# Weaving the FFN's activations and residual in 16-byte chunks

## The reference

```python
x = x + merged @ w_o                                   # D_MODEL = 2048
h = rmsnorm(x, norm_ffn_g)
z = h @ w_up                                           # D_FF = 5632, two halves
a, v = z[..., :D_FF], z[..., D_FF:]
ext = jnp.concatenate([buf, a], axis=1)                # buf: the last 2 rows
conv = conv_b + sum(conv_w[k] * ext[:, k:k + T] for k in range(3))
x = x + (jax.nn.silu(conv) * v) @ w_down
y = rmsnorm(x, norm_final_g)
```

## Time and profile before

| | us |
|---|---|
| median of 3 runs | 1944.33 (1944.02 to 1944.99) |
| the profiled execution | 1944.88 |
| its span, first to last instruction | 1943.1 |
| PE busy | 1927.0 (99%) |
| DVE busy | 1091.2 (56%) |
| ACT busy | 760.4 (39%) |
| POOL busy | 96.4 (5%) |

### The profile page before, as it was taken

The page is one execution under the profiler, slowest core; times in us unless marked ns, Lnnn a source line. Parts: engine busy times, 40 slices in busy tenths (PEclk is TensorE's granted clock), DMA queues, the critical chain, the costliest instruction groups (busy, mean ns, idle before and its releaser), DMA issues.

```text
span 1943.1 us, 34161 instructions
## 1 busy us (share of the span) xinstructions
PE 1927.0 (99%) x13412; PEld 1909.0 (98%) x13412; DVE 1091.2 (56%) x1506; ACT 760.4 (39%) x846; POOL 96.4 (5%) x252
## 2 busy tenths in 40 slices
PE   9999999999999999999999999999999999999997
PEld 8999999999999999999999999999999999999997
DVE  6865344434345774455556565656656556565656
ACT  5456542332257653333343333332323333333334
POOL 0002000000000350000000000000000000000000
PEclk9999999999999999999999999999999999999999
DMA  7444444444443697454444444434344444443443
GB/s 254 152 152 178 151 151 151 151 151 151 151 173 136 214 312 257 166 205 151 151 159 152 141 163 141 162 140 162 139 163 151 151 151 151 139 163 138 165 145 112
DMA packets 60042, 318.18 MB, mean 164 GB/s; under 512 B 6674, under 2 KB 6994, under 8 KB 27346
## 3 DMA queue, kind: packets, MB, share of 16 engines
q1 hardware_dynamic: 59330, 313.15, 45.0%
q10 hardware_dynamic: 656, 4.27, 0.5%
HBM read 313.08 MB, written 4.32 MB: 163 GB/s over the span
## 4 chain that ended last, share of the span: by engine, by line
PE 93%; DVE 3%; ACT 1%; DMA 1%; issue 1%; SPq 0%; POOL 0%; DVEq 0%; ACTq 0%; POOLq 0%
PE ps L1647 93%; ACT w_hi L583 1%; DVE w_lo L1026 0%; DVE keys_lo L1026 0%; DMA xT<-in_x 0%; DMA w_raw<-in_cache_t 0%; PE ps L1963 0%; DMA c_raw<-in_cache 0%; DVE y_gain L1026 0%; POOL k_rope_all L549 0%; ACT sm L835 0%; DVE sm L1373 0%; SPq L424 0%; SPq L408 0%; PE ps L1913 0%
## 5 line engine op out<-in xcount | busy, mean ns | idle before, releaser
L1026 DVE TENSOR_TENSOR w_lo<-w_raw,w_hi 128x2048 fp32r<-128x2048 f32 (+1 forms) x251 | 571.1, 2276 | 436.9 <-ACT w_hi L583 436.9
L1647 PE MATMUL ps<-h_lo,w_hi 128*128 128x320 f32 x2512 | 768.7, 309 | 0.2 <-DVE h_lo L1118 0.2
L1647 PE MATMUL ps<-h_hi,w_hi 128*128 128x320 f32 x2512 | 756.5, 304 | 0.9 <-ACT w_hi L583 0.7
L583 ACT ACTIVATE w_hi<-w_raw 128x2048 fp32r<-128x2048 f32 (+2 forms) x253 | 479.3, 1895 | 597.4 <-PE ps L1647 585.1
L1647 PE MATMUL ps<-h_hi,w_lo 128*128 128x320 f32 x2496 | 686.5, 307 | 1.4 <-DVE w_lo L1026 1.4
L1647 PEld LDWEIGHTS ps<-h_hi,w_hi 128*128 128x128 f32 x2512 | 471.6, 188 | 2.2 <-ACT w_hi L583 1.2
L1647 PEld LDWEIGHTS ps<-h_lo,w_hi 128*128 128x128 f32 x2512 | 470.1, 187 | 1.0 <-DVE h_lo L1118 0.7
L1647 PEld LDWEIGHTS ps<-h_hi,w_lo 128*128 128x128 f32 x2496 | 448.6, 188 | 1.9 <-DVE w_lo L1026 1.9
L1647 PE MATMUL ps<-hid_lo,w_hi 128*128 128x320 f32 x704 | 217.5, 309 | 0.0
L1647 PE MATMUL ps<-hid_hi,w_hi 128*128 128x320 f32 x722 | 216.3, 303 | 0.0
L1647 PE MATMUL ps<-hid_hi,w_lo 128*128 128x320 f32 x704 | 215.4, 306 | 0.0
(11 more groups left out here) (249 smaller groups left out, 1953.3 us busy)
## 6 DMA issues: line engine op xcount, KB each, us to landing
w_raw<-in_slabs SPq DMA_DIRECT2D x252, 1024.0 KB, 4.8
w_raw<-in_cache_t SPq DMA_DIRECT2D x64, 288.0 KB, 4.2
c_raw<-in_cache SPq DMA_DIRECT2D x56, 256.0 KB, 4.5
w_whole<-in_slabs SPq DMA_DIRECT2D x4, 1024.0 KB, 7.5
x_again<-in_x ACTq DMA_DIRECT2D x1, 2560.0 KB, 9.3
c_last<-in_cache SPq DMA_DIRECT2D x8, 256.0 KB, 4.1
xT<-in_x SPq DMA_DIRECT2D x3, 640.0 KB, 9.5
w_raw<-in_slabs SPq DMA_DIRECT2D x3, 512.0 KB, 8.3
```

The costliest lines, as they stand in the source:

```text
L583: return nc.scalar.activation(out, in_, ACT.Copy)
L1026: return nc.vector.tensor_tensor(out, a, b, op)
L1647: return nc.tensor.matmul(out, a, b, start=start, stop=stop, **kw)
```

## The change

`h2_hi`, `h2_lo` and `x1` become three lanes of one tile: 4 words (16 bytes) of the first, 4 of the second, 4 of the third, and so on along the row. `hid_hi`, `hid_lo` and `hid32` likewise; `hid32` has four tiles in place of two. Every instruction that reads or writes them gets the corresponding access pattern of 80 runs of 4 words, 48 bytes apart; a partner that lies consecutively is only seen in fours as well. `cv` moves to another region, since the woven `hid` is longer. No instruction, wait or DMA is added or removed.

```diff
+LANES = 3
...
-        x1 = sb("x1", [P, KD, T], at=qn_reg)
+        x1 = sb("x1", [P, KD, T // 4, LANES, 4], at=r1)[:, :, :, 2, :]
...
-        h2_hi = sb("h2_hi", [P, KD, T], F32R, at=r1)
-        h2_lo = sb("h2_lo", [P, KD, T], F32R, at=r1 + TB)
-        hid_hi = sb("hid_hi", [P, FPC, T], F32R, at=a_reg)
-        hid_lo = sb("hid_lo", [P, FPC, T], F32R, at=a_reg + FPC * T * 4)
-        aext = sb("aext", [P, 2, CEXT], at=a_reg + 2 * FPC * T * 4)
-        cv = sb("cv", [P, 3, CEXT], at=a_reg + 13312)
+        h2 = sb("h2", [P, KD, T // 4, LANES, 4], F32R, at=r1)
+        h2_hi, h2_lo = h2[:, :, :, 0, :], h2[:, :, :, 1, :]
+        hid = sb("hid", [P, FPC, T // 4, LANES, 4], F32R, at=a_reg)
+        hid_hi, hid_lo = hid[:, :, :, 0, :], hid[:, :, :, 1, :]
+        hid32 = sb("hid32", [P, FPC, T // 4, LANES, 4], at=a_reg)[:, :, :, 2, :]
+        aext = sb("aext", [P, 2, CEXT], at=a_reg + FPC * LANES * T * 4)
+        cv = sb("cv", [P, 3, CEXT], at=b_reg + 4096)
         silu = sb("silu", [P, 2, CEXT], at=b_reg)
-        hid32 = sb("hid32", [P, 2, T], at=b_reg + 4096)
...
+        def fours(t):
+
+            return t.rearrange("p (n c) -> p n c", c=4)
...
-                nc.scalar.activation(h2_hi[:, bass.ds(k, 1), :], x1[:, bass.ds(k, 1), :], ACT.Copy,
+                nc.scalar.activation(h2_hi[:, bass.ds(k, 1), :, :], x1[:, bass.ds(k, 1), :, :], ACT.Copy,
...
-                        copy(hid_hi[:, f, :], hid32[:, f % 2, :]).then_inc(hd_hi, 1)
+                        copy(hid_hi[:, f, :, :], hid32[:, f, :, :]).then_inc(hd_hi, 1)
...
-                        nc.vector.tensor_tensor(hid32[:, f % 2, 0:NP], ps[:, vb, 0:NP], silu[:, f % 2, CW - 1:CPS],
-                                                ALU.mult)
+                        nc.vector.tensor_tensor(hid32[:, f, 0:NP // 4, :], fours(ps[:, vb, 0:NP]),
+                                                fours(silu[:, f % 2, CW - 1:CPS]), ALU.mult)
...
-                        tt(hid_lo[:, f, :], hid32[:, f % 2, :], hid_hi[:, f, :], ALU.subtract).then_inc(hd_lo, 1)
+                        tt(hid_lo[:, f, :, :], hid32[:, f, :, :], hid_hi[:, f, :, :], ALU.subtract).then_inc(hd_lo, 1)
...
-                            tt(x1[:, k, :], ps[:, bank, 0:T], x1[:, k, :], ALU.add).then_inc(dn_taken, 1)
+                            tt(x1[:, k, :, :], fours(ps[:, bank, 0:T]), x1[:, k, :, :], ALU.add).then_inc(dn_taken, 1)
...
-                         [(ps[:, 2 * (f % 2) + s, 0:T], [(wb(k), h2_hi[:, k, :], h2_lo[:, k, :]) for k in range(KD)])],
+                         [(ps[:, 2 * (f % 2) + s, 0:T], [(wb(k), h2_hi[:, k, :, :], h2_lo[:, k, :, :]) for k in range(KD)])],
...
-                        mm(out, blk(w_hi[s], w), hid_hi[:, k, :], k == 0, False)
-                        mm(out, blk(w_hi[s], w), hid_lo[:, k, :], False, False)
-                        last = mm(out, blk(w_lo[s], w), hid_hi[:, k, :], False, k == FPC - 1)
+                        mm(out, blk(w_hi[s], w), hid_hi[:, k, :, :], k == 0, False)
+                        mm(out, blk(w_hi[s], w), hid_lo[:, k, :, :], False, False)
+                        last = mm(out, blk(w_lo[s], w), hid_hi[:, k, :, :], False, k == FPC - 1)
```

More of the change, by code:

```diff
@@ L235, in program, with fours_of @@
         ps = ctx.enter_context(nc.psum_tensor("ps", [P, 8, 512], F32))
+        def fours(t):
+            return t.rearrange("p (n c) -> p n c", c=4)
+        def fours_of(t):
+            return t.rearrange("p a (n c) -> p a n c", c=4)
         def col(name, i):
@@ L945, in take_o @@
                 act.wait_ge(slab_taken, i * 2 + (G0["w_o"] + s + 1))
-                nc.scalar.activation(h2_hi[:, bass.ds(k, 1), :], x1[:, bass.ds(k, 1), :], ACT.Copy,
+                nc.scalar.activation(h2_hi[:, bass.ds(k, 1), :, :], x1[:, bass.ds(k, 1), :, :], ACT.Copy,
                                      scale=vec[:, bass.ds(i * 2 + (s + VEC["g_ffn"]), 1)]).then_inc(h_hi_r[2], 1)
-                nc.scalar.activation(sq[:, bass.ds(k, 1), :], x1[:, bass.ds(k, 1), :], ACT.Square).then_inc(sq_done[2], 1)
+                nc.scalar.activation(fours_of(sq[:, bass.ds(k, 1), :]), x1[:, bass.ds(k, 1), :, :], ACT.Square).then_inc(sq_done[2], 1)
             steps("w_o", take_o, take_first=True)
@@ L956, in end_square @@
                 act.wait_ge(dn_taken, 16 * NCH + k + 1)
-                nc.scalar.activation(sq[:, k, :], x1[:, k, :], ACT.Square).then_inc(end_sq, 1)
+                nc.scalar.activation(fours(sq[:, k, :]), x1[:, k, :, :], ACT.Square).then_inc(end_sq, 1)
             def with_gain(k):
-                nc.scalar.activation(yg[:, k, :], x1[:, k, :], ACT.Copy, scale=col("g_fin", k)).then_inc(end_gain, 1)
+                nc.scalar.activation(fours(yg[:, k, :]), x1[:, k, :, :], ACT.Copy, scale=col("g_fin", k)).then_inc(end_gain, 1)
             def next_hi(c, l):
@@ L1504, in take_o @@
                 dve.wait_ge(slab_used, i * 2 + (G0["w_o"] + s + 1))
-                tt(x1[:, bass.ds(k, 1), :].rearrange("p a t -> p (a t)"), ps[:, s, 0:T],
-                   x_again[:, bass.ds(k, 1), :].rearrange("p a t -> p (a t)"), ALU.add).then_inc(slab_taken, 1)
+                tt(x1[:, bass.ds(k, 1), :, :].rearrange("p a n c -> p (a n) c"), fours(ps[:, s, 0:T]),
+                   fours(x_again[:, bass.ds(k, 1), :].rearrange("p a t -> p (a t)")), ALU.add).then_inc(slab_taken, 1)
                 acc_add(2, k)
                 dve.wait_ge(h_hi_r[2], i * 2 + (s + 1))
-                nc.vector.scalar_tensor_tensor(out=h2_lo[:, bass.ds(k, 1), :], in0=x1[:, bass.ds(k, 1), :],
+                nc.vector.scalar_tensor_tensor(out=h2_lo[:, bass.ds(k, 1), :, :], in0=x1[:, bass.ds(k, 1), :, :],
                                                scalar=vec[:, bass.ds(i * 2 + (s + VEC["g_ffn"]), 1)],
-                                               in1=h2_hi[:, bass.ds(k, 1), :], op0=ALU.mult, op1=ALU.subtract
+                                               in1=h2_hi[:, bass.ds(k, 1), :, :], op0=ALU.mult, op1=ALU.subtract
                                                ).then_inc(h_lo_r[2], 1)
@@ L1542, in chunk @@
                         dve.wait_ge(slab_used, g + 1)
-                        nc.vector.tensor_tensor(hid32[:, f % 2, 0:NP], ps[:, vb, 0:NP], silu[:, f % 2, CW - 1:CPS],
-                                                ALU.mult)
[L1545 to L1548, removed]
+                        nc.vector.tensor_tensor(hid32[:, f, 0:NP // 4, :], fours(ps[:, vb, 0:NP]),
+                                                fours(silu[:, f % 2, CW - 1:CPS]), ALU.mult)
+                        tt(hid32[:, f, NP // 4:, :].rearrange("p (b u) c -> p b u c", b=NB),
+                           ps[:, vb, NP:T].rearrange("p (b u c) -> p b u c", b=NB, c=4),
+                           silu[:, f % 2, CPS:].rearrange("p (b t) -> p b t", b=NB)[:, :, CW - 1:]
+                           .rearrange("p b (u c) -> p b u c", c=4), ALU.mult).then_inc(hd_32, 1)
                         dve.wait_ge(hd_32, c * FPC + (f + 1))
                         dve.wait_ge(hd_hi, c * FPC + (f + 1))
-                        tt(hid_lo[:, f, :], hid32[:, f % 2, :], hid_hi[:, f, :], ALU.subtract).then_inc(hd_lo, 1)
+                        tt(hid_lo[:, f, :, :], hid32[:, f, :, :], hid_hi[:, f, :, :], ALU.subtract).then_inc(hd_lo, 1)
                     if l >= 8:
@@ L2150, in keep_clock @@
                 for k in range(n):
-                    mm(ps[:, 2, 0:T], blk(w_hi[1], k % KD), hid_hi[:, k % FPC, :], True, True)
+                    mm(ps[:, 2, 0:T], blk(w_hi[1], k % KD), hid_hi[:, k % FPC, :, :], True, True)
             keep_clock(4)
```

## The result

The changed kernel takes 1954.65 us, the one before 1944.33 us: ratio 1.0053, 95% interval 1.0041 to 1.0064, 10.3 us slower. I had forecast 1944.3 us and no change as the likeliest, with 1943 to 1947 as its own range, and gave "slower" 0.28.

What follows compares the result with a forecast made beforehand. PE's gapless matmul stream was taken as the bound. The span of 1943.1 us plus 1.8 around it gave 1944.9, every change term was 0, and the runs' median, 0.6 less, made the forecast 1944.3 us, range 1943 to 1947.

Steps and rivals of the forecast that it cites:

- The bound: In the part the change touches, only PE sets the time: 200.00 us busy in a stretch of 200.
- rival 2: DVE and ACT pay by the word for woven operands and PE waits: about +12 us, 1956 us; chance 0.08.
- the places: Moving cv, hid32's four buffers and x1's new place hold up no wait: cost 0.
- The reading of aext: DVE's write of aext in runs of 8 words, 216 ns, was taken to show that eight jumps cost nothing.
- The excess: FFN matmuls take 11.1 ns over their 320 columns at 2.4 GHz; claimed to go with the columns, 8% of them.
- the price of a jump: Cost of 80 jumps in each of 6336 woven FFN matmuls: bounded between 0 and +507 us, taken as 0.
- The lines: SBUF is read in 16-byte lines, two hits cover the latency; the woven operand's four hits cost 0.
- Rival 1: The moving stream of the 6336 matmuls pays for each jump: slower, +70 us, +211 us or 2451 us; chance 0.20.
- Rival 3: The matmuls' excess shrinks as a stride of three lines spreads them: 1874 us if all goes, 1909 if half; chance 0.12.
- the lever argument: Measurement tells 0.2%, 3.9 us, from no change: 0.61 ns for a woven matmul or 0.008 ns for a jump.

Runs made afterwards that it cites:

- flat_fours: Changed kernel with every lane flat again, but cv and hid32 at their new places and hid32 with four buffers: 1944.46 us, ratio 0.9999.
- run_two: Changed kernel with woven runs of 2 words (8 bytes) in place of 4: 2839.28 us.
- The probes: Kernels with blocks of further matmuls behind the end, results unused, to read each block's spacing; flat took 146.6 ns a matmul at 320 columns.
- lo_shifted: Kernel before, all flat, with hid_lo moved by 16 bytes: 1948.83 us, ratio 1.0023.
- lo_third: Changed kernel with lanes reordered to hi, residual, lo, so lo starts 32 bytes behind hi in place of 16: 1943.53 us, ratio 0.9996.
- the grid: Kernel before plus blocks of 36 matmuls, hi and lo each starting 0 to 28 words on: flat 144.4 to 148.9 ns, woven 142.2 to 148.9.
- the triples: Added blocks repeating hi with w_hi, lo with w_hi, hi with w_lo: 144.4 ns flat, 146.7 woven, 144.5 woven with hi in lo's place.
- the probe: Kernel before plus 15 blocks of 208 matmuls, each with another access pattern: flat 146.6 ns, woven 145.3, runs of 2 words 283.3.
- hid_moved: lo_third with woven hid also 64 bytes further on, lo first, product second, hi third: 1940.14 us, ratio 0.9979.
- probe_places: Kernel before plus flat blocks with 128 to 32 weight columns, and with tiles or weights moved 4 words: the moved ones 144.4 to 148.9 ns.

## Why the prediction was wrong

**The bound: right.** PE sets the time, without a gap, before and after.

**ACT and DVE (rival 2), the places: right.** Nothing there changed by more than 2 ns; flat_fours has the places alone at ratio 0.9999. The reading of aext, that short runs cost DVE nothing, holds, but its working showed nothing: a rate and a start-up were taken from two durations and then gave one of the two, 216 ns, back. run_two is the test, with runs of 2 words: the addition to x1 took 491 ns (487 woven in 4, 486 flat), h_lo 564 (547 woven and flat); on ACT h_hi took 601 ns (562 woven, 564 flat).

**The excess: the step that failed first.** "144.4/320 is 0.451 ns a column, 231.1/512 is 0.451 too. The excess goes with the columns." Two points and a chance agreement. The probes give 13.3 ns at 320 and 13.4 to 13.8 at 512, and 13.3 and 13.4 at 256 and 384 (16.0 at 448): it is a fixed cost for each matmul. The value projection's 17.8 ns would then be another value of it, for other operands at other starts; no run tested that. The Trainium skill (TensorE: Matmul & The Clock Gate, "Wait — 56ns, not 53.3ns?") has an excess that is the same for every size. I held two rows against it, and the form of its rule was right; its 2.5 ns are not what these float32r matmuls show (10 to 16 ns here for flat and three-lane streams).

**"I take 0": the price of a jump.** I had the right place and took 0 for it, and jumps in lanes of 16 bytes three apart do cost 0: woven and flat are alike at 512 columns. The failed step is that I asked *only* for the price of a jump. The change also moved lo's start from the same position in a 128-byte grid as hi's to 16 bytes behind it, since lane 1 starts one chunk on. I had that written down as a lane number and gave it no term. Its price is 2.1 to 2.2 ns a matmul inside the slabs, 1.8 ns on average, 11 us; the term is 6336 x (1.8 ns for the start), where I had 6336 x 0. In a flat FFN only the down slabs were tried (lo_shifted); for the up slabs it rests on lo_third, the grid and the triples.

**The lines.** The Trainium skill (Advanced Engine Details and Errata, SBUF Cachelines) asks for at least two hits in a 16-byte line. For 4 hits the traces agree, at three lanes: no cost. For 2 hits they do not: runs of 2 words take 283 ns in the probe and 285 in run_two, nearly twice the flat 146.6, little less than runs of 1 word (290). For PE, of the widths tried here, only runs that fill the 16 bytes keep the rate.

**The rivals.** Rival 1 named the place, the matmuls, and the sign. The mechanism in it (each jump) is refuted by lo_shifted and lo_third together. Rival 2 had 1956 us, 1.4 us from the measurement; that is chance, since none of its parts took place. Rival 3 said a better layout might exist; it does, but for 4 us and not 70.

**The chances.** 0.28 for slower was fair as a number, but it was spread over prices up to +500 us, while the lever argument in the text ("0.61 ns for a woven matmul") already said how little was needed. With 6336 identical instructions on the bound, "no change" demands an argument that excludes half a nanosecond, and I had none.

**What stays open.** What the fixed cost is. It takes values from 10 to 16 ns in flat and three-lane streams of one pattern and 7 to 15 from start to start in the FFN before (140.0 after hi, 148.3 after lo, 145.0 after w_lo), it depends on the starts of consecutive moving operands and on the weights' start, and at 320 columns not on the weight columns; other engines' traffic does not make the loss. In flat streams of one pattern it does not depend on the data either; in woven ones that is open. Nor is it known why the up slabs of hid_moved are faster than those of lo_third. No run here shows the mechanism.

## What to carry to other kernels

When a kernel is bound by thousands of equal matmuls, list for each changed operand its start address as well as its pattern; moving one operand by 16 bytes was worth 2.2 ns a matmul in a kernel whose pattern did not change at all. Before calling an excess proportional, measure it at more than two sizes. And where a layout is to be chosen, a probe with blocks of matmuls behind the kernel's end sorts the candidates cheaply, but its winner has to be timed in place.

## What the hardware showed beyond that

- Moving operand of float32r, 320 columns: runs of 4 words, 32 or 48 bytes apart, as fast as flat in a uniform stream (146.6 and 145.3 ns against 146.6); 64 and 128 bytes apart 153.3 and 156.7; runs of 2 words 283.3; single words in 4 290.0.
- The spacing of a matmul of 320 columns does not fall with fewer weight columns: 146.67 ns with 128, 96, 64 and 32. At 512 columns it is 227.3 ns with 128 weight columns and 230.0 with 64 (probe_places). At 256 columns it is 120.0 ns flat, 117.8 woven.
- An operand that starts 8 bytes off the 16-byte grid costs nothing in a uniform stream: 146.7 ns.
